# Last slices of the output chunk tile by tile, seam gate slices on VectorE, and an opening in one-slice stages

## The chip, the cores and the metric

The kernel runs on one core of a Trainium2 chip. TensorE multiplies, VectorE and ScalarE work on elements, GpSimd and SyncE issue DMAs. The metric is the device time of one execution in microseconds; lower is better. The order of work on each engine is fixed in the program; engines wait for each other at semaphores.

## The reference

One denoising step of a two-layer backbone on 384 tokens: 128 context tokens and 256 latent tokens, model width 2048, all in float32. Both kinds of token share the weights, and differ in the conditioning vector:

```
mod = SiLU(cond) @ w_ada[l] + b_ada[l] -> shift, scale, gate
h   = RMSNorm_pre(x) * (1 + scale) + shift
p   = h @ w_in[l]                       (5120 columns)
l=0: windowed attention with sink, and a 2-D DFT mixing
l=1: multi-scale pooling, and chunked spatial gating
every branch * SiLU(its gate path), concatenated: o (2048 wide)
x   = x + gate * RMSNorm_post(o @ w_out[l])
```

The outputs are the new x of both kinds of token, and the keys and values of the context tokens in layer 0.

## The kernel before, in words

**Tiles and chunks.** The tokens are three tiles of 128 (t = 0 to 2). The product is worked off in 28 chunks of 512 output columns (`CHUNKS`): per layer ten of w_in and four of w_out ("out" chunks; those are chunks 10 to 13 and 24 to 27). Layer 1 begins at chunk L1 = 14. A chunk takes 16 k-steps, one for each slice of 128 rows (`KT`). A weight is split in a high and a low half of its bits: ScalarE rounds (`round_half`, L938, writes `w_hi`), VectorE subtracts (`split_half`, L1147, writes `w_lo`), for two slices at a time, called a half. A k-step is nine products, three for each tile (L732 to L734), into the accumulator bank of that tile; `mm_done` counts halves. `w_hi` and `w_lo` are rings of three halves. The loop of the k-step takes all three tiles within a step, so the three tiles of a chunk are complete together.

**The timetable.** `timetable()` writes down by hand at which place (chunk, step) every other piece of work stands, and each engine goes through the same list of places. At a place TensorE does the k-step and then the entries; ScalarE and VectorE do the entries and then the round or the split of the half that lies two ahead (from chunk 3 on; in the opening the round and split stand first). `pre` entries stand ahead of a chunk. Side products (transposes of h, the gate rows, and so on) take turns in two spare banks. SyncE loads the weights in the order of `loads`, through a ring `raw` of four slots of 1 MB; a load waits until the one four before it has been used, and everything behind waits too.

**The opening.** Chunks 0 to 2 (v, k, q) run interleaved, as h comes slice by slice. h needs the scale and shift columns of its slice, which come from a product of `w_ada` with the condition: eight stages (`STAGES`) of two slices, each of four entries `first_ada` (L754, one load of 1 MB in runs of 256 columns for scale and for shift, ring of three slots), transposed by `first_cols` (L761), and then `h`: transposes on TensorE (L800), scale and shift on ScalarE (L1006), its high half (L1010), its low half on VectorE (L1358). Chunks 1 and 2 share a bank set, so their sums are spilled to SBUF at each change (`spill`, 24 times).

**Wide sums.** The gate of layer 0 and the shift of layer 1 are not multiplied on TensorE. VectorE sums them (`wide_sum`, L1313): GpSimd loads half rows of w_ada into two buffers `wide_raw` (L627), each used by two sums; the next load into a buffer waits for both. 64 sums a block, one in 1.3 steps for the gate (from chunk 3 step 10) and one a step for the shift (from chunk 9 step 3). `wide_fold` adds the partitions up at the end.

**The seam.** Between the last out chunk of layer 0 (13) and chunk 14: the shift's transposes `cols` (L791), then for all three tiles the square of the sums (`square_y`, L977), the product with the gate (`evac`, L1443), the mean and root, the `residual` (L1194, twelve pieces of 512 columns), the squares of the new x (L951), the pre-norm (L1177), and h. The gate of layer 1 starts here: slices 0 to 5 (`SEAM_ADA`) are products on TensorE (L693), the other ten are ten loads into `raw` summed on VectorE in two halves (`lane_sum`, L1345, 40 sums, one in 2.5 steps from chunk 15). x is loaded again (`reload`) at step 6 of chunk 13. The end of chunk 27 has the same chain, and then the stores.

Of the kernel before, what the change touches and what calls it, by code (L numbers as in the profile page):

```python
# [29 lines left out]
P = 128  # L30
D = 2048
# [31 lines left out]
L1 = PER_LAYER  # L63

# [6 lines left out]
SEAM_ADA = 6  # L71
# [9 lines left out]
STAGES = 8  # L81

WIDE = [(GATE_BLOCK[0], FIRST, 10, 13, 10), (SHIFT_BLOCK, FIRST + 6, 3, 1, 1)]
# [3 lines left out]
HALVES = [half for q in range(4) for half in (  # L87
    [(1, 0), (0, 0), (1, 1), (0, 1), (2, 0), (2, 1)] if q == 0 else
    [(0, 2 * q), (1, 2 * q), (1, 2 * q + 1), (0, 2 * q + 1), (2, 2 * q), (2, 2 * q + 1)])]
HALVES += [(c, h) for c in range(FIRST, len(CHUNKS)) for h in range(KT // 2)]  # L90
NTH_HALF = {ch: n for n, ch in enumerate(HALVES)}
QUARTERS = []
for c_, h_ in HALVES:
    if (c_, h_ // 2) not in QUARTERS:
        QUARTERS.append((c_, h_ // 2))
NTH_QUARTER = {cq: n for n, cq in enumerate(QUARTERS)}
# [12 lines left out]
def timetable():  # L109
# [12 lines left out]
    steps = [(c, 2 * h + i) for c, h in HALVES[:FIRST * KT // 2] for i in range(2)]  # L122

    def first(n, *entry):
        put(*steps[n], *entry)

    pre(0, "square")
    for i in range(4):
        pre(0, "first_ada", 0, i)
        if i == 1:  # L130
            pre(0, "norm")
    pre(0, "first_weights")
    pre(0, "first_cols", 0)
    for k in range(2):
        pre(0, "h", 0, k)
    for i, n in enumerate((0, 1, 2, 2)):
        first(n, "first_ada", 1, i)
    first(3, "first_cols", 1)
    for k in range(2, 4):
        first(3, "h", 0, k)  # L140
    for b in range(2, STAGES):
        at_ = 12 * (b // 2 - 1) + 4
        ada, cols, h = ((0, 1, 2, 4), 5, 6) if b % 2 == 0 else ((5, 6, 7, 8), 9, 10)
        for i in range(4):
            first(at_ + ada[i], "first_ada", b, i)
        first(at_ + cols, "first_cols", b)
        for k in range(2 * b, 2 * b + 2):
            first(at_ + h, "h", 0, k)
    for c in SPILLED:
        for q in range(4):  # L150
            for t in range(TOKS):
                put(c, 4 * q + 3, "spill", c, q, t)

    pre(L1, "cols", SHIFT_BLOCK)
    for t in range(TOKS):
# [11 lines left out]
    for c, (layer, kind, _) in enumerate(CHUNKS):  # L167
        nxt = c + 1
        if kind == "out":

            for n in range(2):
                put(c, 10 + 2 * n, "gate_y", c, n)
            if c not in (L1 - 1, 2 * L1 - 1):
                for t in range(TOKS):
                    put(nxt, t, "evac", c, t)
            continue
        step = {"k": 3, "q": 3, "vd": 2}.get(kind, 1)
        if c == KEPT:

            for t in range(TOKS):  # L180
                put(FIRST - 1, 12 + t, "evac", c, t)
            continue
        if c == SPILLED[0]:

            for n, t in ((-2, 1), (0, 2)):
                first(len(steps) - 4 + n, "evac", c, t)
            for n, t in ((-1, 0), (0, 1), (2, 2)):
                first(len(steps) - 4 + n, "turn", c, t)
            continue
# [40 lines left out]
    for half in range(2):  # L230
        for i in range(SUM_LOADS):
            for j in range(4):
                n = 4 * (SUM_LOADS * half + i) + j
                put(L1 + 1, 5 * n // 2, "lane_sum", half, i, j // 2, j % 2)
        put(L1 + 1, 10 * SUM_LOADS * (half + 1) + 2, "fold", half)
    put(10, 5, "cols", SCALE_BLOCK)
    end = len(CHUNKS)
    for t in range(TOKS):
        pre(end, "evac", end - 1, t)
    pre(end, "residual", 1)  # L240
# [8 lines left out]
def places():  # L249
    yield ("pre", 0)  # L250
    for c, h in HALVES:
        if h == 0 and c >= FIRST:
            yield ("pre", c)
        for s in range(2 * h, 2 * h + 2):
# [4 lines left out]
def hybrid_step(nc, x_prompt, x_sample, cond_cols, w_ada, first_cols, ada_rows, norm_rows, w_in, w_out, cache_kt,  # L259
# [10 lines left out]
    loads, fetched = [], 2  # L270
    for p in places():
        if p[0] == "at" and p[2] % 2 == 0:
            n = NTH_HALF[p[1], p[2] // 2] + (3 if p[1] < FIRST else 2)
            if n < len(HALVES):
                c, h = HALVES[n]
# [1350 lines left out]
```

## Time and profile before

| | |
|---|---|
| median of 3 runs | 1205.12 us (1203.51 to 1207.18) |
| the profiled execution | 1205.11 us |
| its span, first to last instruction | 1203.3 us |
| TensorE busy | 1136.3 us, 94% |
| VectorE busy | 694.0 us, 58% |
| ScalarE busy | 421.5 us, 35% |
| mean granted TensorE clock | 0.987 of full speed |
| DMA | 235.97 MB, mean 196 GB/s |

The time of an execution is the span and about 1.8 us around it. An engine that is busy is not an engine at its peak: a product counts as busy while it waits in TensorE's pipeline. "Idle before" in a row, in square brackets, is the time that the engine stood still ahead of that instruction, and what released it. Times in a timeline are counted from the start of the span.

### The profile page before, as it was taken

The page shows a single profiled execution, that of the slowest core. Times are in us where ns is not written, and L with a number is a line of the kernel's source. Part 1 is how long each engine was busy: PE and PEld are TensorE (multiplying, and loading weights), DVE is VectorE, ACT ScalarE, POOL GpSimd, SP SyncE. Part 2 cuts the span into 40 slices and gives each one's busy share as a digit, 9 for nine tenths or more (in the row PEclk, how much of TensorE's full clock was granted, in tenths as well). Part 3 has the DMA queues.
Part 4 walks back from the last instruction along what each step waited for, and adds up shares of the span by engine and source line. Part 5 has one row for each costly group of instructions (what it writes and reads, how often), then busy time and mean ns, then how long its engine had stood idle before and what let it go on. Part 6 is the DMA issues. An engine that isn't in the chain of part 4 may idle for free.

```text
span 1203.3 us, 13779 instructions
## 1 busy us (share of the span) xinstructions
PE 1136.3 (94%) x5404; PEld 876.3 (73%) x5404; DVE 694.0 (58%) x949; ACT 421.5 (35%) x653; POOL 50.9 (4%) x98
## 2 busy tenths in 40 slices
PE   3799999999999999999999699999999999999994
PEld 0456677877787877777777388888788878878883
DVE  3354555678788784688873553466665643243333
ACT  3323234333455342233332673223233323242331
POOL 1000010000000001011111000000000000000000
PEclk9999999999999999999999799999999999999998
DMA  9998974655565576666678534444344633433413
GB/s 329 328 315 295 301 253 151 227 202 196 180 245 210 183 263 245 210 215 222 221 241 310 226 106 146 150 158 161 125 173 171 209 114 131 140 105 107 138 35 105
DMA packets 113056, 235.97 MB, mean 196 GB/s; under 512 B 5280, under 2 KB 38080, under 8 KB 109408
## 3 DMA queue, kind: packets, MB, share of 16 engines
q1 hardware_dynamic: 100976, 190.86, 46.1%
q0 software_dynamic: 11440, 41.08, 10.3%
q10 hardware_dynamic: 576, 3.16, 0.7%
q8 instruction: 43, 0.70, 0.2%
q14 instruction: 21, 0.17, 0.0%
HBM read 231.40 MB, written 3.67 MB: 195 GB/s over the span
## 4 chain that ended last, share of the span: by engine, by line
PE 82%; DMA 7%; DVE 6%; issue 2%; ACT 2%; SPq 0%; DVEq 0%; ACTq 0%
PE bank L732 23%; PE bank L734 22%; PE bank L733 22%; DMA wide_raw<-in_w_ada 5%; PE bank L754 3%; DVE wide L1313 2%; DVE w_lo L1147 2%; PE bank L856 1%; DVE x L1194 1%; PE bank L693 1%; DMA raw_first<-in_w_ada 1%; PE bank L839 1%; DMA raw<-in_w_in 1%; PE bank L901 1%; PE bank L800 1%
## 5 line engine op out<-in xcount | busy, mean ns | idle before, releaser
L732 PE MATMUL bank<-w_hi,h_op 128*128 128x512 f32 x1152 | 474.7, 412 | 7.2 <-DVE h_op L1358 4.2
L734 PE MATMUL bank<-w_hi,h_op 128*128 128x512 f32 x1152 | 452.9, 393 | 0.0
L733 PE MATMUL bank<-w_lo,h_op 128*128 128x512 f32 x1152 | 451.6, 392 | 0.0
L1147 DVE TENSOR_TENSOR w_lo<-raw,w_hi 128x1024 fp32r<-128x1024 f32 x224 | 272.9, 1221 | 196.6 <-ACT w_hi L938 196.3
L938 ACT ACTIVATE w_hi<-raw 128x1024 fp32r<-128x1024 f32 x224 | 234.7, 1054 | 244.5 <-PE bank L734 233.0
L732 PEld LDWEIGHTS bank<-w_hi,h_op 128*128 128x128 f32 x1152 | 217.8, 189 | 87.3 <-issue 40.5
L734 PEld LDWEIGHTS bank<-w_hi,h_op 128*128 128x128 f32 x1152 | 217.5, 189 | 48.6
L733 PEld LDWEIGHTS bank<-w_lo,h_op 128*128 128x128 f32 x1152 | 218.2, 189 | 40.5 <-issue 0.7
L1313 DVE SCALAR_TENSOR_TENSOR wide<-wide_raw,cond,wide 128x1024 f32<-128x1024 f32 x120 | 152.3, 1276 | 20.0 <-DMA wide_raw<-in_w_ada 19.8
L732 PE MATMUL bank<-w_hi,o_low 128*128 128x512 f32 x192 | 76.9, 400 | 3.1 <-DVE w_lo L1147 3.0
L734 PE MATMUL bank<-w_hi,o_low 128*128 128x512 f32 x192 | 74.9, 390 | 0.0
L733 PE MATMUL bank<-w_lo,o_low 128*128 128x512 f32 x192 | 74.9, 390 | 0.0
L754 PE MATMUL bank<-raw_first,cond 128*32 128x512 f32 x256 | 38.0, 672 | 22.0 <-DMA raw_first<-in_w_ada 19.8
L1006 ACT ACTIVATE silu<-bank,shift_t,scale_t 128x128 f32<-128x128 f32 x64 | 29.1, 505 | 67.6 <-PE bank L800 58.3
L627 POOL DMA_DIRECT2D wide_raw<-in_w_ada x64 | 33.9, 530 | 363.0 <-DVE wide L1313 330.4
L732 PEld LDWEIGHTS bank<-w_hi,o_low 128*128 128x128 f32 x192 | 36.0, 188 | 14.2 <-DVE w_lo L1147 6.5
L1345 DVE SCALAR_TENSOR_TENSOR lanes<-raw,cond,lanes 128x1024 f32<-128x1024 f32 x36 | 46.0, 1278 | 0.0
L1358 DVE TENSOR_TENSOR h_op<-silu,h_op 128x384 fp32r<-128x384 f32 x32 | 17.9, 558 | 47.8 <-ACT h_op L1010 47.8
L734 PEld LDWEIGHTS bank<-w_hi,o_low 128*128 128x128 f32 x192 | 36.0, 188 | 7.7
L733 PEld LDWEIGHTS bank<-w_lo,o_low 128*128 128x128 f32 x192 | 36.1, 188 | 6.9
L1025 ACT ACTIVATE probs_t<-bank 128x384 f32<-128x384 f32 (+1 forms) x36 | 15.1, 419 | 64.8 <-PE bank L846 64.6
L1032 ACT ACTIVATE probs<-bank,neg_max 128x384 f32<-128x384 f32 (+1 forms) x36 | 18.4, 511 | 50.9 <-DVE neg_max L1381 50.9
(181 smaller groups left out, 755.6 us busy)
## 6 DMA issues: line engine op xcount, KB each, us to landing
raw<-in_w_in SPq DMA_DIRECT2D x80, 1024.0 KB, 6.7
raw_first<-in_w_ada SPq DMA_DIRECT2D x64, 512.0 KB, 6.2
raw<-in_w_ada SPq DMA_DIRECT2D x32, 1024.0 KB, 5.7
wide_raw<-in_w_ada POOLq DMA_DIRECT2D x64, 512.0 KB, 4.3
raw<-in_w_out SPq DMA_DIRECT2D x32, 1024.0 KB, 5.1
x<-in_x_sample SPq DMA_DIRECT2D x2, 1024.0 KB, 9.7
x<-in_x_sample ACTq DMA_DIRECT2D x2, 1024.0 KB, 11.4
out_y_sample<-x SPq DMA_DIRECT2D x8, 256.0 KB, 3.1
```

The lines of the kernel that those rows point to most:

```text
L627: pool.dma_start(wide_raw[:, i % 2, :], w_ada[layer, k * P:(k + 1) * P, col:col + LANES])\
L732: pe.matmul(out, operand(layer, kind, 0, k, t), hi, start=k % group == 0, stop=False)
L733: pe.matmul(out, operand(layer, kind, 0, k, t), lo, start=False, stop=False)
L734: last = pe.matmul(out, operand(layer, kind, 1, k, t), hi, start=False, stop=k % group == group - 1)
L754: last = pe.matmul(out[32 * j:32 * j + 32, :], cond[:, 4 * i + j, :], raw_first[:, slot, CW * j:CW * (j + 1)], start=True, stop=True)
L938: act.activation(w_hi[:, half % WRING, :, :].rearrange("p k n -> p (k n)"), src, ACT.Copy)\
L1006: last = act.activation(full[:, lo_:hi_], side_bank(e)[:, lo_:hi_], ACT.Identity, bias=shift_t[:, k, c_:c_ + 1], scale=scale_t[:, k, c_:c_ ...
L1032: freed(act.activation(probs[:, 0:n], side_bank(e)[:, 0:n], ACT.Exp, bias=neg_max[:, u:u + 1], scale=SCALE, accum_out=row_sum[:, u:u + 1]), e)
L1147: dve.tensor_tensor(w_lo[:, half % WRING, :, :].rearrange("p k n -> p (k n)"), src, hi, ALU.subtract)\
L1313: dve.scalar_tensor_tensor(out=wide[:, c_, cols], in0=src, scalar=cond[:, k, c_:c_ + 1], in1=wide[:, c_, cols], op0=ALU.mult, op1=ALU.add)\
L1345: dve.scalar_tensor_tensor(out=lanes[:, c_, :], in0=src, scalar=factor, in1=lanes[:, c_, :], op0=ALU.mult, op1=ALU.add).then_inc(lane_summ ...
L1358: dve.tensor_tensor(h_op[:, 1, k, :], h_full[k % 2], h_op[:, 0, k, :].bitcast(F32), ALU.subtract)\
```

## The change

Four things are changed.

1. *Opening.* The first two slices have a stage each, so there are nine stages: `[0], [1], [2, 3], ...`. A stage of one slice has two entries, each of eight slices of w_ada and 128 columns for scale and shift; they multiply 256 columns instead of 512. Weights of chunks 0 to 2 are loaded by halves (`UNITS`, 512 KB, one slot of `raw` each). The order within a round of two slices is chunk 2, 0, 1 and 1, 0, 2 in turn; the first round goes slice by slice. There are 27 spills (`STAYS`). The order of the first loads is written out. The norm stands before the first entry, and a Sqrt on ScalarE between the squares of x loads its table early.
2. *Wide sums.* The gate block takes one sum in 1.2 steps; the shift block begins at chunk 8 step 13 and takes one in 1.1 steps.
3. *Last slices.* In chunks 13 and 27 the last four slices are multiplied tile by tile: `tile_steps` does 12 products of tile 0 at step 12, of tile 1 at 13, of tile 2 at 14. It counts `y_done`. Squares, gate product, root and residual are entries for each tile, and in chunk 13 so are the squares of x. The gate rows come at steps 7 and 9 instead of 10 and 12, the Sqrt table at step 10, the shift's `cols` at step 8 of chunk 13. The rounds and splits of the first two halves of chunk 14 are entries of their own.
4. *Seam gate.* `SEAM_ADA` is 2: two slices on TensorE, and 14 in 14 loads and 56 lane sums, one in 2.25 steps.

```diff
-SEAM_ADA = 6
+SEAM_ADA = 2
-WIDE = [(GATE_BLOCK[0], FIRST, 10, 13, 10), (SHIFT_BLOCK, FIRST + 6, 3, 1, 1)]
+WIDE = [(GATE_BLOCK[0], FIRST, 10, 12, 10), (SHIFT_BLOCK, FIRST + 5, 13, 11, 10)]
+STAGES = [[0], [1]] + [[2 * r, 2 * r + 1] for r in range(1, ROUNDS)]
+OPENING = [(2, 0), (0, 0), (2, 1), (0, 1), (1, 0), (1, 1)]
+OPENING += [(c, 2 * r + i) for r in range(1, ROUNDS) for c in round_order(r) for i in range(2)]
...
     pre(0, "square")
+    pre(0, "norm")
+    pre(0, "first_ada", 0, 0)
+    pre(0, "norm_rest")
+    pre(0, "first_ada", 0, 1)
     pre(0, "first_cols", 0)
+    pre(0, "first_weights", 0)
+    pre(0, "h", 0, 0)
+    pre(0, "first_weights", 1)
+    pre(0, "first_ada", 1, 0)
+    first(0, "first_ada", 1, 1)
+    first(1, "first_cols", 1)
+    first(1, "h", 0, 1)
+    for n, i in ((1, 0), (1, 1), (3, 2), (4, 3)):
+        first(n, "first_ada", 2, i)
+    first(4, "first_cols", 2)
...
+    for b in range(3, len(STAGES)):
+        at_ = 6 * (b - 2)
         for i in range(4):
+            first(at_ - 1 + i, "first_ada", b, i)
+        first(at_ + 3, "first_cols", b)
+        for k in STAGES[b]:
+            first(at_ + 4, "h", 0, k)
...
-    pre(L1, "cols", SHIFT_BLOCK)
-    for t in range(TOKS):
-        pre(L1, "evac", L1 - 1, t)
-    pre(L1, "residual", 0)
+    put(L1 - 1, 8, "cols", SHIFT_BLOCK)
+    after = [NTH_HALF[L1, h] for h in range(2)]
+    for layer, c in enumerate(LAST):
+        put(c, 10, "table", c)
+        put(c, 12, "y_square", c, 0)
+        put(c, 12, "y_mix", c, 0)
+        put(c, 12, "y_root", layer, 0)
+        put(c, 12, "residual", layer, 0)
+        put(c, 13, "y_square", c, 1)
+        if layer == 0:
+            put(c, 13, "round", after[0])
+        put(c, 13, "y_mix", c, 1)
+        put(c, 14, "y_root", layer, 1)
+        put(c, 14, "residual", layer, 1)
+        put(c, 14, "y_square", c, 2)
+        put(c, 14, "y_mix", c, 2)
+        if layer == 0:
+            pre(c + 1, "x_square", 0)
+        pre(c + 1, "y_root", layer, 2)
+        pre(c + 1, "residual", layer, 2)
+    pre(L1, "x_square", 1)
+    pre(L1, "round", after[1])
+    pre(L1, "x_square", 2)
+    pre(L1, "x_norm")
+    pre(L1, "xn", 1, 0)
     pre(L1, "ada", GATE_BLOCK[1], 0, SEAM_ADA)
-    pre(L1, "xn", 1, 0)
-    for k in range(3):
+    pre(L1, "split", after[0])
+    pre(L1, "h", 1, 0)
+    pre(L1, "split", after[1])
+    for k in range(1, 3):
         pre(L1, "h", 1, k)
...
-                put(c, 10 + 2 * n, "gate_y", c, n)
+                put(c, (7 if c in LAST else 10) + 2 * n, "gate_y", c, n)
...
+            def tile_steps(c, t):
+                layer, kind, _ = CHUNKS[c]
+                out = acc(c, t)[:, :]
+                for k in range(KT - 4, KT):
+                    half = NTH_HALF[c, k // 2]
+                    hi = w_hi[:, half % WRING, k % 2, :]
+                    lo = w_lo[:, half % WRING, k % 2, :]
+                    pe.matmul(out, operand(layer, kind, 0, k, t), hi, start=False, stop=False)
+                    pe.matmul(out, operand(layer, kind, 0, k, t), lo, start=False, stop=False)
+                    last = pe.matmul(out, operand(layer, kind, 1, k, t), hi, start=False, stop=k == KT - 1)
+                    if t == TOKS - 1 and k % 2:
+                        last.then_inc(mm_done, 1)
+                if t < TOKS - 1:
+                    last.then_inc(y_done, 1)
...
+                if c in LAST and k >= KT - 4:
+                    if k == KT - 4:
+                        pe.wait_ge(lo_ready, half + 2)
+                    if k < KT - 1:
+                        tile_steps(c, k - (KT - 4))
+                    return
```

## Rows read from the trace of the kernel before

**Rows 1.** The page: the span, and its busy time by engine.
```profile
span 1203.3 us, 13779 instructions
...
PE 1136.3 (94%) x5404; PEld 876.3 (73%) x5404; DVE 694.0 (58%) x949; ACT 421.5 (35%) x653; POOL 50.9 (4%) x98
```

**Rows 2.** Waits of TensorE, whole span: total us, times, longest us.
```profile
PE bank L732 <- DVE w_lo L1147: 5.9, 9, 2.0
```

**Rows 3.** Timeline, TensorE (start, us, instruction): gate product, chunks 10, 13, 24, 27.
```profile
536.21 0.49 PE L814 MATMUL bank<-gate_parts,row_sel_r 32*128 32x512 f32 x1
...
648.92 0.49 PE L814 MATMUL bank<-gate_parts,row_sel_r 32*128 32x512 f32 x1
...
1074.21 0.49 PE L814 MATMUL bank<-gate_parts,row_sel_r 32*128 32x512 f32 x1
...
1176.12 0.49 PE L814 MATMUL bank<-gate_parts,row_sel_r 32*128 32x512 f32 x1
```

**Rows 4.** Chain of waits, 500 to 660 us: start us, us, what.
```profile
514.37 6.37 DMA wide_raw<-in_w_ada
...
597.39 1.22 DVE w_lo L1147
598.61 1.21 DVE wide L1313
600.10 6.70 DMA wide_raw<-in_w_ada
...
619.86 5.21 DMA wide_raw<-in_w_ada
```

**Rows 5.** Timelines of TensorE and ScalarE at the seam.
```profile
660.36 0.60 PE L791 MATMUL bank<-ident,rows 128*128 128x128 f32 x4
...
661.22 1.28 ACT L975 ACT_TABLE_LOAD   x1
662.51 0.20 ACT L975 ACTIVATE junk<-stat 128x3 f32<-128x3 f32 x1
...
676.25 0.19 ACT L951 ACTIVATION_READ_ACCUMULATOR mixed<-x 128x1 f32 x1
...
681.90 0.77 PE L732 MATMUL bank<-w_hi,h_op 128*128 128x512 f32 x1 [0.34 <-DVE h_op L1358]
```

**Rows 6.** Timeline of the end of the last chunk and the tail.
```profile
1178.28 1.23 DVE L1147 TENSOR_TENSOR w_lo<-raw,w_hi 128x1024 fp32r<-128x1024 f32 x1 [5.80 <-ACT w_hi L938]
...
1187.33 0.39 PE L734 MATMUL bank<-w_hi,h_op 128*128 128x512 f32 x1
...
1188.83 2.13 DVE L1443 TENSOR_TENSOR mixed<-bank,silu 128x512 f32<-128x512 f32 x3 [9.32 <-ACT junk L977]
...
1191.72 8.04 DVE L1194 SCALAR_TENSOR_TENSOR x<-mixed,stat,x 128x512 f32<-128x512 f32 x12
```

**Rows 7.** Timeline of the opening.
```profile
16.58 1.94 PE L754 MATMUL bank<-raw_first,cond 128*32 128x512 f32 x8 [16.58 <-DMA raw_first<-in_w_ada]
...
25.59 1.94 PE L754 MATMUL bank<-raw_first,cond 128*32 128x512 f32 x8 [1.06 <-DMA raw_first<-in_w_ada]
...
28.20 1.06 ACT L938 ACTIVATE w_hi<-raw 128x1024 fp32r<-128x1024 f32 x1 [2.56 <-DMA raw<-in_w_in]
...
30.92 1.06 ACT L938 ACTIVATE w_hi<-raw 128x1024 fp32r<-128x1024 f32 x1 [1.66 <-DMA raw<-in_w_in]
...
36.04 0.76 PE L732 MATMUL bank<-w_hi,h_op 128*128 128x512 f32 x1 [1.75 <-DVE h_op L1358]
```

**Rows 8.** Timeline of TensorE, later in the opening: entry products.
```profile
79.03 1.06 PE L754 MATMUL bank<-raw_first,cond 128*32 128x512 f32 x8 [0.72 <-ACT silu L1006]
...
82.29 1.07 PE L754 MATMUL bank<-raw_first,cond 128*32 128x512 f32 x8
...
154.11 1.07 PE L754 MATMUL bank<-raw_first,cond 128*32 128x512 f32 x8 [0.72 <-ACT silu L1006]
```

**Rows 9.** Waits of TensorE from 700 to 1190 us.
```profile
PE bank L732 <- DVE w_lo L1147: 0.5, 1, 0.5
```

More of the change, by code:

```diff
@@ L118, in pre @@
         at.setdefault(("pre", c), []).append(entry)
-    steps = [(c, 2 * h + i) for c, h in HALVES[:FIRST * KT // 2] for i in range(2)]
     def first(n, *entry):
-        put(*steps[n], *entry)
+        put(*OPENING[n], *entry)
     pre(0, "square")
[L128 to L132, printed above, removed]
-    pre(0, "first_cols", 0)
[L134 to L137, printed above, removed]
@@ L180, in timetable @@
             for t in range(TOKS):
-                put(FIRST - 1, 12 + t, "evac", c, t)
+                put(FIRST - 1, 14 + t // 2, "evac", c, t)
             continue
         if c == SPILLED[0]:
[L185 to L188, printed above, removed]
+            first(-4, "evac", c, 1)
+            first(-3, "turn", c, 0)
+            first(-2, "evac", c, 2)
+            first(-2, "turn", c, 1)
+            put(FIRST, 0, "turn", c, 2)
             continue
@@ L233, in timetable @@
                 n = 4 * (SUM_LOADS * half + i) + j
-                put(L1 + 1, 5 * n // 2, "lane_sum", half, i, j // 2, j % 2)
-        put(L1 + 1, 10 * SUM_LOADS * (half + 1) + 2, "fold", half)
+                put(L1 + 1, 9 * n // 4, "lane_sum", half, i, j // 2, j % 2)
+        put(L1 + 1, 9 * SUM_LOADS * (half + 1) + 2, "fold", half)
     put(10, 5, "cols", SCALE_BLOCK)
[L237 to L240, printed above, removed]
     return at
@@ L250, in places @@
     yield ("pre", 0)
[L251 to L254, printed above, removed]
+    for c, s in OPENING:
+        yield ("at", c, s)
+    for c in range(FIRST, len(CHUNKS)):
+        yield ("pre", c)
+        for s in range(KT):
             yield ("at", c, s)
@@ L266, in hybrid_step, with opening_loads @@
     assert len(nth_side) == len(side)
-    loads, fetched = [], 2
+    def opening_loads():
+        yield from (("first_ada", 0, 0), ("first_ada", 0, 1), ("mm", 0), ("mm", 1))
+        yield from (("first_ada", 1, 0), ("first_ada", 1, 1), ("mm", 2))
+        yield from (("first_ada", 2, 0), ("first_ada", 2, 1), ("mm", 3), ("first_ada", 2, 2), ("first_ada", 2, 3))
+        yield from (("mm", 4), ("mm", 5), ("first_ada", 3, 0))
+        for b in range(3, len(STAGES)):
+            for i in range(1, 4):
+                yield ("mm", 3 * (b - 1) + i - 1)
+                yield ("first_ada", b, i)
+            if b + 1 < len(STAGES):
+                yield ("first_ada", b + 1, 0)
+    loads = list(opening_loads())
+    fetched = 3 * ROUNDS
     for p in places():
@@ L287, in hybrid_step @@
                 loads.append(("sum", e[1], e[2]))
-    assert [x[1] for x in loads if x[0] == "mm"] == list(range(len(QUARTERS)))
+    assert [x[1] for x in loads if x[0] == "mm"] == list(range(len(UNITS)))
+    assert [x for x in loads if x[0] == "first_ada"] == [e for e in side if e[0] == "first_ada"]
     nth_first = {x: n for n, x in enumerate(x for x in loads if x[0] == "first_ada")}
@@ L498, in half_ahead @@
         def half_ahead(p):
-            if p[0] == "at" and p[2] % 2:
+            if p[0] == "at" and p[2] % 2 and p[1:] not in ((L1 - 1, KT - 3), (L1 - 1, KT - 1)):
                 half = NTH_HALF[p[1], p[2] // 2] + 2
@@ L1510, in part @@
                     norm_x(0)
-                    for j in range(PIECES):
+                    norm_piece(0)
+                elif what == "norm_rest":
+                    for j in range(1, PIECES):
                         norm_piece(j)
```

278 lines of the change are left out of this document (156 added, 122 removed).

## The prediction

> **What bounds the kernel now.** I read the page first: the span is 1203.3 us [rows 1], and the profiled execution's own time is 1205.11 us, so 1.8 us lie outside the span; the median of the three runs is 1205.12, the same. I add everything against 1205.1. TensorE holds 94% of the span [rows 1], so only stretches in which it stands still or is pushed apart can pay. The list of what TensorE waits for [rows 2] names one inside the steady run: `w_lo`, the low half of a weight split, late from VectorE, 5.9 us in nine waits. The list shows no more of it, because products that run one by one behind late weight loads count as busy; the rate shows the whole.
>
> The steady rate comes from TensorE's timeline [rows 3]. The gate product after step 10 of an output chunk recurs in layer 1 from 1074.21 to 1176.12 over three chunks: 33.97 us a chunk. Two gate products cost about 0.5 each, so a k-step is 2.06 us, and a third of four steps (one tile's share) 2.75. In layer 0 the same three intervals take 648.92 - 536.21 = 112.71 us: 10.8 more. The fold of the shift block (about 2.1) is work; 8.7 is loss, and some 0.9 is lost just before 536. So **9.6 us** go at the wide sums of the shift block. Why: the chain of waits [rows 4] runs there 12 times, from 514.37 to 619.86, through the same ring: load, sum, split, sum, next load. 11 turns take 105.5 us, 9.6 each; less two sums (1.28 each), a split (1.22) and about 0.5 of latencies, 5.3 us are left for a load; a turn holds four sums, placed one a step, for which TensorE would want only 4 x 2.12 = 8.5.
>
> The two other losses are read from the timelines: the seam, from the last product of layer 0 (660.36) to the first of layer 1 (681.90), 21.5 us [rows 5], and the tail, from 1187.56 (1187.33 plus one spacing of 0.23) to the end of the span, 15.7 us [rows 6]. In both, ScalarE and VectorE do a serial chain after all three tiles are complete. The opening takes 36.04 us to the first main product [rows 7].
>
> **Opening.** Four entries of one megabyte, then two of w_in, land before the first product. Entries with 1 KB runs land 9.01/3 = 3.00 us apart (16.58 to 25.59), w_in with 2 KB runs 2.72 apart [rows 7]. The new first stage needs two entries and two half-megabyte loads. Its entries have 512-byte runs, which no row shows. A price per byte plus one per packet through the two rows gives 0.28 us for 512 packets more, and for 1024 more 0.6: 3.6 us an entry. Lower bound 3.0 (runs cost nothing), upper bound 6.0 (all cost is per packet). I take 3.6, as going from 2 KB to 1 KB shows so little. The Trainium skill's "DMA: Bandwidth & Descriptors", under Specifications, gives 512 B as the smallest transfer at line rate; by it the entries cost 3.0 and the opening gains up to 2.6 us more. No run shown here decides it.
>
> x is in at 16.6 - 3.0 = 13.6. Entries at 17.2 and 20.8, two weight halves (1.36 each) 23.5, third entry 27.1. The third entry's product stands in TensorE's order ahead of the first k-step and takes 2.0 us, so the first step begins at 29.1; the h chain is done by 27. That is 7 us earlier. Then the loads set the pace: fourth entry 30.7, a weight half 32.1, stage 2's entries at 35.1, 38.1, 42.5, 45.5, two halves 48.2, and stage 3's at 51.2, 55.6, 60.0 and 64.3. TensorE waits about 1 us at each of the last three. Its product ends at 65.4; three steps with their column and h transposes and one more entry product (3 x 2.06, 1.1, 1.0 and 0.2 behind each fp32 group) put the thirteenth step at about 74. Before, it follows the product at 82.29, at 83.4 [rows 8]. But 13 entries are done by then instead of 15: two more at 1.2 us each remain. The waits of 0.72 us for ScalarE, one at each odd stage [rows 8], lie at an h transpose with no step behind it; the new order puts a step there, and the two that fall after step 12 go. 9.4 - 2.4 + 1.4 = 8.4; with small slips for three more spills I take **8.0** (2 to 11). A round needs 16.1 us of loads and had 75.08/4 = 18.8 us of TensorE, so after stage 3 the loads fall behind no more. Half-size weight loads leave four halves in the ring, over 16 us of work, so the ring costs nothing.
>
> **Shift block.** It starts at chunk 8 step 13 instead of chunk 9 step 3, one sum in 1.1 steps, and ends at the same place. Four sums then have 4.4 x 2.12 = 9.3 us. The turn of 9.6 comprises two sums, one split between them and the load. The new places alternate in blocks of ten sums: even sums on odd steps, where the split falls between, and on even ones, where it follows and the turn is 1.2 shorter, 8.4. The mean, 9.0, fits; the odd blocks overrun by 0.3 a turn, which the two halves of lead absorb. So the stall goes but for 0.6: **9.0** (4 to 9.6). The gate block of layer 0 goes from 1.3 to 1.2 steps a sum; that costs some VectorE room in the attention stage and perhaps 0.3.
>
> **Last four slices by tile.** TensorE's work is the same, in other order. Count from its end, T. Tile 0 is complete at T - 5.5, tile 1 at T - 2.75. Before, VectorE's product follows T by 1.27 us [rows 6]: square and its latency. A tile on VectorE now costs reduce and scale 0.36, product 0.71, reciprocal 0.2, residual 8.04/3 = 2.68: 3.95. Tile 0 runs from -4.2 to -0.25; tiles 1 and 2 queue behind it to 3.7 and 7.7. Before, the residual ended at 1199.76, T + 12.2: 4.5 us gained. What follows (the last 256 KB out, 3.5 us) stays.
>
> A price comes with it. TensorE now wants both halves 6 and 7 split before step 12, at T - 8.24. The gate products move to steps 7 and 9. After the second (0.4 before step 10, T - 12.8) ScalarE has to empty it, round half 6, load the Sqrt table and use it (661.22 to 662.71, 1.5 [rows 5]), and only then round half 7. Round 7 waits behind these on ScalarE, VectorE's split behind round 7, TensorE behind the split. Before, the split of half 7 ended 3.39 us after the gate product (1176.12 to 1179.51 [rows 3, 6]); with one round more (1.06 [rows 7]) and the table it ends 5.95 after, at T - 6.85. TensorE stands for 1.4 us, in both last chunks (bounds 0, if ScalarE gets ahead, and 3). ScalarE's next instruction starts 0.01 us behind a table load here [rows 5]. The Trainium skill's "ScalarE: Activation LUTs", under What ACT_TABLE_LOAD costs, adds a drain of 1380 ns to the load of 1283; by it the stall would be 2.8 us, and the whole sum 2.8 us worse. The trace has the load at 1.28 and no room for the drain, and I go by the trace.
>
> Tail: 4.5 - 1.4 = 3.1, taken as **3.0** (1 to 5).
>
> Seam: the residual is done at 7.7; ScalarE squares tile 1 from 4.3 to 6.4, rounds a half to 7.5, squares tile 2 in two halves to 9.9. From the end of the last square to the first product took 681.90 - 676.44 = 5.46 [rows 5]; one small add more (0.2), and the 0.6 evacuation of the gate block now comes after the norm pieces. First product at T + 15.0 instead of 21.5: 6.5. Off go 1.4 of stall and 0.6 for the shift's transposes [rows 5], which lay in the gap and now lie among the steps. **4.5** (1 to 6). The gate block's products at the seam fall from six slices to two. They ran inside the gap, hidden behind the residual; in the shorter gap six would have ended at about 12 and been next in line, so that move earns nothing alone, but protects the 4.5. x's reload, issued at the same step 6, has to have landed by T - 2.8.
>
> **Sixteen more lane sums** (1.28 each, 20.5 us) go to VectorE in chunks 15 to 22, one per 2.25 steps. VectorE is 58% busy over the span [rows 1] and TensorE waited 0.5 us for splits in all after 700 [rows 9], so they cost perhaps 0.5.
>
> Sum: 8.0 + 9.0 + 3.0 + 4.5 - 0.8 = 23.7; 1205.1 - 23.7 = 1181.4.
>
> **Rivals.**
> *The runs of 512 bytes are dear.* At 6.0 an entry the first four cost 9.6 more: 1191. For it: the opening is paced by loads. Against: 1 KB costs only a tenth more than 2 KB. 0.12.
> *The shift block still starves.* If the load, not the placing, sets the turn (9.6 against 9.3 of cover, loads up to 6.7 [rows 4]), half or all of the 9 stays: 1186 to 1190. 0.16.
> *The tiles gain nothing.* The late half 7, or x late, eats the seam and tail: 1186 to 1189. 0.08.
> *Everything fits better:* entries at 3.0, ScalarE ahead: 1176. 0.09.
> *Slower.* The ring of `raw`: a sum load holds one of four slots for 6.75 steps until its fourth sum, and SyncE's queue waits behind it. There are 14 instead of 10. If each kept the weights back for 2 us, 28 us would go in chunks 15 to 22, and 1209 would result; from that price on it decides. Against: the load behind it is wanted some 5 steps, 10 us, later, and with ten such loads TensorE waited 0.5 us in all [rows 9]. 0.04. No change that can be told, because several of these meet: 0.04.
> The forecast itself: 0.47.
>
> 0.3% is 3.6 us, about what this kernel's measurement tells from no change. Faster 0.91, same 0.04, slower 0.05 (the ring and an unseen thing). Range: the likeliest alone is 1177 to 1186; with the dear runs, the starving block and the better case, 1173 to 1192.
>
> **What would show it.** First main product near 29 us instead of 36; thirteenth step near 74. Three gate intervals in layer 0 of about 104 us instead of 112.7, and the wide loads gone from the chain. A gap of about 15 us at the seam, a tail of about 11.2 after the last product, and a pause of 1 to 2 us before step 12 of both last chunks, waiting for `w_lo`. The forecast is wrong if entries of the first stages land over 4.5 us apart, if the chain still runs through `wide_raw`, or if the last residual begins later than T + 6.

## The result and the profile after

The changed kernel takes 1184.87 us (median of 4 runs, 1183.69 to 1185.8), the kernel before 1204.32 beside it (4 runs, 1200.76 to 1207.18). The ratio is 0.9839 [0.9811, 0.9868]: 19.5 us, 1.6% less. The profiled executions, by which everything below goes, have spans of 1203.3 and 1181.6 us, 21.7 apart.

The page after, span and busy time by engine (before: [rows 1]):

```profile
span 1181.6 us, 13864 instructions
...
PE 1126.5 (95%) x5404; PEld 876.4 (74%) x5404; DVE 715.6 (61%) x985; ACT 421.4 (36%) x660; POOL 50.9 (4%) x98
```

TensorE is busy 9.8 us less. Of this 5.4 lie in the gap at the seam, where four slices of the gate fewer are multiplied, 3.4 in the opening and 2.5 between the gate product of chunk 10 and the end of chunk 13; elsewhere it is busy 1.4 more. The other 12 us are idle time that went.

What TensorE waits for, whole span (total us, times, longest us); before the only row of the steady run was [rows 2]:

```profile
PE bank L838 <- DMA raw_first<-in_w_ada: 24.8, 10, 16.9
PE bank L884 <- DVE mixed L1276: 8.6, 1, 8.6
PE bank L814 <- DVE w_lo L1243: 2.6, 3, 2.0
PE bank L769 <- DVE w_lo L1243: 2.6, 2, 1.3
```

Row 1 is the opening, row 2 the seam. In row 3, L814 is a k-step's product, and one wait of 2.0 us in chunk 18 is most of it; in row 4, L769 is the first product of `tile_steps`, and each of its two waits is one of 1.3 us.

TensorE's timeline at the landmarks (start, us, instruction, idle before and its releaser): the opening, the gate product of chunks 10, 11, 12 and 13, the last chunk of layer 0, the seam, one wait in chunk 18, and the last chunk.

```profile
16.94 1.94 PE L838 MATMUL bank<-raw_first,cond 128*32 128x256 f32 x16 [16.94 <-DMA raw_first<-in_w_ada]
20.44 1.94 PE L838 MATMUL bank<-raw_first,cond 128*32 128x256 f32 x16 [1.57 <-DMA raw_first<-in_w_ada]
...
28.75 0.80 PE L814 MATMUL bank<-w_hi,h_op 128*128 128x512 f32 x1
...
72.38 1.07 PE L838 MATMUL bank<-raw_first,cond 128*32 128x512 f32 x8
...
139.18 1.06 PE L838 MATMUL bank<-raw_first,cond 128*32 128x512 f32 x8 [0.65 <-DMA raw_first<-in_w_ada]
...
530.99 0.49 PE L898 MATMUL bank<-gate_parts,row_sel_r 32*128 32x512 f32 x1
...
564.95 0.49 PE L898 MATMUL bank<-gate_parts,row_sel_r 32*128 32x512 f32 x1
...
598.92 0.49 PE L898 MATMUL bank<-gate_parts,row_sel_r 32*128 32x512 f32 x1
...
640.22 0.47 PE L769 MATMUL bank<-w_hi,h_op 128*128 128x512 f32 x1 [1.30 <-DVE w_lo L1243]
...
648.56 1.92 PE L752 MATMUL bank<-raw,cond 128*32 128x512 f32 x16
...
662.29 0.77 PE L814 MATMUL bank<-w_hi,h_op 128*128 128x512 f32 x1 [0.34 <-DVE h_op L1469]
...
864.78 0.50 PE L814 MATMUL bank<-w_hi,h_op 128*128 128x512 f32 x1 [2.05 <-DVE w_lo L1243]
...
1162.84 0.47 PE L769 MATMUL bank<-w_hi,h_op 128*128 128x512 f32 x1 [1.27 <-DVE w_lo L1243]
```

The first product stands at 28.75 instead of 36.04 [rows 7]. The gate products of the shift block are 33.96 and 33.97 us apart, the rate of layer 1 before. Layer 0 ends at T = 648.47 (last tile product and one spacing) instead of 660.36 [rows 5], and the first product of layer 1 follows 13.8 us later instead of 21.5. The last product ends at 1171.13, 10.5 us before the end of the span; before, 15.7 [rows 6]. The waits in square brackets at 640.22, 864.78 and 1162.84 are time that the changed kernel lost anew.

Put end to end, the 21.7 us of span are (T is the end of the last product of layer 0):

| stretch | before | after | gain |
|---|---|---|---|
| to the start of the last spill, taken as the end of the opening | 187.81 | 181.15 | 6.7 |
| to the gate product of chunk 10 | 348.40 | 349.84 | -1.4 |
| to the end T of chunk 13 | 124.15 | 117.48 | 6.7 |
| T to first product of layer 1 | 21.54 | 13.82 | 7.7 |
| layer 1 to its last product | 505.66 | 508.84 | -3.2 |
| tail | 15.74 | 10.47 | 5.3 |

The tiles at the seam, VectorE's timeline of chunk 13's end:

```profile
638.85 1.23 DVE L1243 TENSOR_TENSOR w_lo<-raw,w_hi 128x1024 fp32r<-128x1024 f32 x1 [1.39 <-ACT w_hi L1022]
...
645.26 2.74 DVE L1300 SCALAR_TENSOR_TENSOR x<-mixed,stat,x 128x512 f32<-128x512 f32 x4
...
649.08 2.74 DVE L1300 SCALAR_TENSOR_TENSOR x<-mixed,stat,x 128x512 f32<-128x512 f32 x4
...
652.91 2.74 DVE L1300 SCALAR_TENSOR_TENSOR x<-mixed,stat,x 128x512 f32<-128x512 f32 x4
```

The residuals of the three tiles stand 3.8 us apart, tile 0's before T, the last one done at 655.65, T + 7.2. At the end of the last chunk it is the same, and there the one residual of 8.04 us ended at T + 12.2 before [rows 6].

### The profile page after: what moved, and what is told of

Same layout as the page of the kernel before. It is cut to its first block, busy times and chain, and to the rows that moved or that the text cites. A ratio compares the mean times of both kernels' runs of the same rounds, so it can differ in the third digit from the quotient of the medians.

```text
span 1181.6 us, 13864 instructions
## 1 busy us (share of the span) xinstructions
PE 1126.5 (95%) x5404; PEld 876.4 (74%) x5404; DVE 715.6 (61%) x985; ACT 421.4 (36%) x660; POOL 50.9 (4%) x98
## 4 chain that ended last, share of the span: by engine, by line
PE 81%; DVE 5%; DMA 5%; ACT 4%; issue 3%; SPq 2%; DVEq 0%; ACTq 0%
PE bank L814 23%; PE bank L816 23%; PE bank L815 23%; DMA raw_first<-in_w_ada 4%; DVE w_lo L1243 2%; PE bank L940 1%; SPq L615 1%; PE bank L752 1%; ACT w_hi L1022 1%; ACT silu L1087 1%; DVE x L1300 1%; PE bank L838 1%; PE bank L923 1%; PE bank L985 1%; PE bank L890 1%
## 5 line engine op out<-in xcount | busy, mean ns | idle before, releaser
L814 PE MATMUL bank<-w_hi,h_op 128*128 128x512 f32 x1128 | 464.7, 412 | 3.1 <-DVE w_lo L1243 2.6
L816 PE MATMUL bank<-w_hi,h_op 128*128 128x512 f32 x1128 | 443.8, 393 | 0.0
L815 PE MATMUL bank<-w_lo,h_op 128*128 128x512 f32 x1128 | 442.3, 392 | 0.0
L814 PEld LDWEIGHTS bank<-w_hi,h_op 128*128 128x128 f32 x1128 | 213.2, 189 | 79.9 <-issue 35.3
L816 PEld LDWEIGHTS bank<-w_hi,h_op 128*128 128x128 f32 x1128 | 212.7, 189 | 46.9
L815 PEld LDWEIGHTS bank<-w_lo,h_op 128*128 128x128 f32 x1128 | 213.6, 189 | 39.8 <-issue 0.7
L814 PE MATMUL bank<-w_hi,o_low 128*128 128x512 f32 x192 | 75.9, 396 | 0.0
L1456 DVE SCALAR_TENSOR_TENSOR lanes<-raw,cond,lanes 128x1024 f32<-128x1024 f32 x52 | 66.4, 1277 | 0.0
L838 PE MATMUL bank<-raw_first,cond 128*32 128x512 f32 (+1 forms) x288 | 36.8, 598 | 25.1 <-DMA raw_first<-in_w_ada 24.8
L1087 ACT ACTIVATE silu<-bank,shift_t,scale_t 128x128 f32<-128x128 f32 x64 | 29.1, 505 | 80.3 <-PE bank L884 60.9
L1469 DVE TENSOR_TENSOR h_op<-silu,h_op 128x384 fp32r<-128x384 f32 x32 | 17.9, 558 | 43.2 <-ACT h_op L1091 43.2
L814 PEld LDWEIGHTS bank<-w_hi,o_low 128*128 128x128 f32 x192 | 36.1, 188 | 8.0 <-issue 0.8
```

What stands on the lines that cost most here:

```text
L814: pe.matmul(out, operand(layer, kind, 0, k, t), hi, start=k == begin, stop=False)
L815: pe.matmul(out, operand(layer, kind, 0, k, t), lo, start=False, stop=False)
L816: last = pe.matmul(out, operand(layer, kind, 1, k, t), hi, start=False, stop=k == end)
L838: last = pe.matmul(out[32 * j:32 * j + 32, 0:n_], cond[:, ks * i + s, :], raw_first[:, slot, n_ * s:n_ * (s + 1)], start=s < 4, stop=s >= ...
L1087: last = act.activation(full[:, lo_:hi_], side_bank(e)[:, lo_:hi_], ACT.Identity, bias=shift_t[:, k, c_:c_ + 1], scale=scale_t[:, k, c_:c_ ...
L1456: dve.scalar_tensor_tensor(out=lanes[:, c_, :], in0=src, scalar=factor, in1=lanes[:, c_, :], op0=ALU.mult, op1=ALU.add).then_inc(lane_summ ...
```

## The experiments

Ten runs. The change's own time was taken a second time among them, as a base for small differences. Where one is compared with the changed kernel, it is with 1184.87 for the first four runs (experiments 1 to 3) and with the second time, 1184.64, for those after it. The kernel before took 1206.52 us beside the first four, 1202.84 beside the next ones and 1203.54 beside the last two, against 1204.32 beside the changed kernel; so a difference of 2 to 3 us between times that were not taken side by side isn't told by them alone, and the profiles are asked where it lies.

**1. The wide sums alone, and all but them.** The kernel before with the new places, and the changed kernel with the old ones:

```diff
-WIDE = [(GATE_BLOCK[0], FIRST, 10, 13, 10), (SHIFT_BLOCK, FIRST + 6, 3, 1, 1)]
+WIDE = [(GATE_BLOCK[0], FIRST, 10, 12, 10), (SHIFT_BLOCK, FIRST + 5, 13, 11, 10)]
```

> The kernel before with the two lines of wide sums of the change alone (gate block one sum in 1.2 steps, shift block from chunk 8 step 13 at one in 1.1). Theory (the turn of load, two sums and a split was longer than four steps, and its slack was the whole loss): the three gate intervals in layer 0 fall from 112.7 to about 104.0 us, the attention stage loses about 1 to 1.5 us, and the time falls by 7 to 8 us. Rival (the load time sets the turn whatever the places): the intervals stay above 110 and the time falls by under 3 us.

> The changed kernel with the wide sums as before (1.3 steps, then from chunk 9 step 3 one a step). Theory: the gate intervals of layer 0 are about 110 to 113 us again, the time from the end of the opening to the first gate product of chunk 10 is 1 to 1.5 us shorter than in the changed kernel, and the time is 6 to 8 us above it. Rival (the lead of the new opening has its own part in the cure): the intervals stay near 104 and the time within 2 us.

Measured: alone 1194.51 us, ratio 0.9905 [0.9884, 0.9927], 12.0 less than the kernel before beside it, where 7 to 8 were expected; undone 1193.01, ratio 0.9896 [0.9869, 0.9923], 8.1 above the changed kernel. Alone, the timeline of TensorE shows the gate products of chunks 10 and 13 at the same step as before:

```profile
534.06 0.49 PE L814 MATMUL bank<-gate_parts,row_sel_r 32*128 32x512 f32 x1
...
638.09 0.49 PE L814 MATMUL bank<-gate_parts,row_sel_r 32*128 32x512 f32 x1
```

104.03 us against 112.71 [rows 3]: 8.7 gained there. Some 2.5 more by the end of the opening is the same opening at 185.36 instead of 187.81, which is scatter. Undone, the changed kernel needs 129.0 us from the gate product of chunk 10 to T instead of 117.5, and gets 1.3 back ahead of that product and 1.0 in layer 1. Of these 11.5 us some 3 are the clock's: behind a wait of 2.53 us it was granted at half speed for about 7 us. So the places themselves are worth 8 to 9 us both ways. TensorE's waits (whole span) have the row back:

```profile
PE bank L814 <- DVE w_lo L1243: 7.5, 6, 2.5
```

So with the same loads the places of the sums decide whether TensorE stalls, and the rival of a block that starves anyway falls from both sides.

**2. Tiles in the step again.** The changed kernel with the entries of each tile, but its products in the old order, so that all tiles are complete together:

```diff
-                if c in LAST and k >= KT - 4:
-                    if k == KT - 4:
-                        pe.wait_ge(lo_ready, half + 2)
-                    if k < KT - 1:
-                        tile_steps(c, k - (KT - 4))
-                    return
...
+                    if c in LAST and k == KT - 1 and t < TOKS - 1:
+                        last.then_inc(y_done, 1)
```

> The changed kernel with the last four slices of chunks 13 and 27 multiplied step by step as before, so that all three tiles are complete in the last step; the entries for each tile stay. Theory (the order of the products is what gains, as VectorE's chain of 3.8 us a tile starts 5.5 us earlier): the tail is 5 us longer than 10.5, the gap at the seam 5 us longer than 13.8, the pauses of 1.3 us before step 12 go, and the time is 7 to 8 us above the changed kernel. Rival (the finer entries gain by themselves, squares of x beside the residual above all): the seam loses less than 3 us and the time less than 4 us.

Measured: 1189.93 us, ratio 0.987 [0.9847, 0.9893], 5.1 slower than the changed kernel, less than the 7 to 8 expected and more than the rival's 4. TensorE's timeline at the seam:

```profile
649.67 0.39 PE L809 MATMUL bank<-w_hi,h_op 128*128 128x512 f32 x1
649.99 1.92 PE L752 MATMUL bank<-raw,cond 128*32 128x512 f32 x16
...
667.80 0.77 PE L807 MATMUL bank<-w_hi,h_op 128*128 128x512 f32 x1 [0.34 <-DVE h_op L1464]
```

The seam gap is 667.80 - 649.90 = 17.9 us (13.8 + 4.1), the tail 14.5 (10.5 + 4.1), and neither `w_lo` pause is there. So of the 7.7 us gained at the seam 4.1 come from the order of the products, and 3.6 from the rest of the change there; at the tail it is 4.1 and 1.2. The 3.6 aren't all the cut in entries: before, the first square of the sums stood behind the shift's transposes and the table load,

```profile
662.75 0.60 ACT L977 ACTIVATE junk<-bank 128x512 f32<-128x512 f32 x1
```

at T + 2.4, while at the tail, where the table was in already, it stood at T + 0.55. In this run it stands at 648.80, T - 1.1, as it waits for its own tile alone. That the transposes and the table left the gap is thus worth up to 1.8 of the 3.6; the two were not tried apart. The order, with the table at step 10, costs two pauses and gives 8.2.

**3. The Sqrt table later.** The changed kernel, the table behind the last round:

```diff
-        put(c, 10, "table", c)
+        put(c, 12, "table", c)
```

> The changed kernel with the Sqrt table loaded at step 12 of chunks 13 and 27, behind the round of half 7, instead of at step 10. Theory (the load of 1.3 us and the small Sqrt stand ahead of that round and make TensorE wait 1.3 us before step 12): both pauses go, seam gap and tail stay as they are, as the table is in before tile 0 is complete; 2.0 to 2.6 us gained. Rival (the gate product at step 9 alone makes the round late): pauses of over 0.8 us stay. Second rival (the load is then in the way of tile 0's square): the tail grows by what the pause gives.

Measured: 1181.44 us, ratio 0.9798 [0.9777, 0.9819], 3.4 faster than the changed kernel, where 2.0 to 2.6 were expected. ScalarE's timeline, of the changed kernel and then of this one:

```profile
634.66 0.60 ACT L1175 ACTIVATE silu<-bank 128x512 f32<-128x512 f32 x1 [2.30 <-PE bank L898]
635.15 1.05 ACT L1022 ACTIVATE w_hi<-raw 128x1024 fp32r<-128x1024 f32 x1
636.22 1.28 ACT L1189 ACT_TABLE_LOAD   x1
637.52 0.20 ACT L1189 ACTIVATE junk<-stat 128x3 f32<-128x3 f32 x1
637.75 1.06 ACT L1022 ACTIVATE w_hi<-raw 128x1024 fp32r<-128x1024 f32 x1
```

```profile
635.27 2.00 ACT L1022 ACTIVATE w_hi<-raw 128x1024 fp32r<-128x1024 f32 x2
637.29 1.28 ACT L1189 ACT_TABLE_LOAD   x1
638.59 0.20 ACT L1189 ACTIVATE junk<-stat 128x3 f32<-128x3 f32 x1
641.99 0.60 ACT L1058 ACTIVATE junk<-bank 128x512 f32<-128x512 f32 x1 [3.20 <-PE bank L771]
```

The two rounds stand together, both pauses are gone, and the table is in 3.2 us before the first square wants it. The seam (13.84) and the tail (10.41) stay as they are. The pauses are 2.6 of the 3.4. Most of the rest is not the table's: layer 1 is 2.3 us shorter, 1.3 of it the pause, and about 0.8 because TensorE's clock didn't fall behind the wait in chunk 18, as it did in both profiles of the changed kernel (see the last section).

**4. The fold before its successors.** The first seven of 14 lane loads are folded by a product on TensorE at place 65 of chunks 15 on; the first sum of the second half stands at place 63:

```diff
-        put(L1 + 1, 9 * SUM_LOADS * (half + 1) + 2, "fold", half)
+        put(L1 + 1, 9 * SUM_LOADS * (half + 1) - 1, "fold", half)
```

> The changed kernel with the fold of each half of the lane sums three steps earlier (at 62 and 125 steps after the start instead of 65 and 128). Theory (the first lane sum of the second half, at step 63, waits for the fold on TensorE at step 65, and the split of that step lies behind it on VectorE, so that TensorE waits 2.05 us at 864.8): that wait goes and the time falls by 2 us. Rival (sixteen more lane sums crowd VectorE): a wait for a late low half of 1 us or more stays in chunks 15 to 23.

> The changed kernel itself, for its time on the same chip as the next three: a ratio of 0.981 to 0.987 to the kernel before, a span near 1182 us.

Measured: 1181.98 us, ratio 0.9825 [0.981, 0.984], against 1184.64, ratio 0.985 [0.9834, 0.9866], for the changed kernel again: 2.7 less. VectorE's timeline of the changed kernel at the wait:

```profile
862.83 0.75 DVE L1454 TENSOR_SCALAR lanes<-raw,cond 128x1024 f32<-128x1024 f32 x1 [10.56 <-issue]
863.50 1.22 DVE L1243 TENSOR_TENSOR w_lo<-raw,w_hi 128x1024 fp32r<-128x1024 f32 x1
```

VectorE stands 10.6 us before the first sum of the second half. The profile names no releaser; by the program it is the fold, as `lanes` may not be written anew before TensorE has read it. The split of the next weights is queued behind the sum, and TensorE, which finishes the wait only by getting to place 65, then lacks that split for 2.05 us. With the fold three steps earlier TensorE's waits from 700 to 1180 us are down to the pause before step 12 of chunk 27:

```profile
PE bank L769 <- DVE w_lo L1243: 1.3, 1, 1.3
```

The crowding by sixteen more sums, the rival, had no part in it, nor had the ring of `raw`: all 14 loads are there still, and the wait is gone. Every time of this run lies below every time of the changed kernel beside it (1180.57 to 1182.71 against 1183.45 to 1186.7). Of the 2.7 us 2.05 are the wait. Some 0.8 are TensorE's clock, which was granted at half speed (1.2 GHz) for 3 us behind that wait in both profiles of the changed kernel. In experiment 5 the wait is there and the clock stays at full speed. Three us of each, 1.2 us behind the restart (us; PE, PEld, VectorE, ScalarE, GpSimd busy; clock, DMA share, GB/s):

```profile
866.00:869.00 3.00, 3.00 (x8) 2.31 (x8) 3.00 (x5) 0.96 (x2) 0.00 (x0) 0.51 0.93 316
```

```profile
863.36:866.36 3.00, 3.00 (x14) 2.46 (x14) 3.00 (x5) 0.97 (x2) 0.00 (x0) 1.00 0.90 315
```

It is 8 products against 14 in the same time.

**5. Entries ahead of the weights.** In the opening SyncE issues three entries of a stage each behind a weight half. Turned round:

```diff
-                yield ("mm", 3 * (b - 1) + i - 1)
                 yield ("first_ada", b, i)
+                yield ("mm", 3 * (b - 1) + i - 1)
```

> The changed kernel with entries 1 to 3 of stages 3 to 8 each loaded ahead of the weight half with which they are paired, instead of behind it. Theory (SyncE's queue stands at the weight half, which waits for a slot of the ring of four half-filled slots, and the entries behind it start late): the waits of TensorE for an entry in stages 4 to 8 (0.2 to 0.65 us each, 2.1 in all) go, and the time falls by about 2 us. Rival (the DMA engines are full, and any order gives the same): the waits stay at 2 us in sum or move to the weights.

Measured: 1180.25 us, ratio 0.9812 [0.9798, 0.9826], 4.4 less than the changed kernel, where about 2 were expected. SyncE's timeline, of the changed kernel and of this one (L648 a weight half, L615 an entry, in two DMAs):

```profile
66.83 0.37 SPq L648 DMA_DIRECT2D raw<-in_w_in  x1
67.24 1.02 SPq L615 DMA_DIRECT2D raw_first<-in_w_ada  x2
75.19 0.37 SPq L648 DMA_DIRECT2D raw<-in_w_in  x1
```

```profile
66.53 1.42 SPq L648 DMA_DIRECT2D raw<-in_w_in  x1
72.39 0.92 SPq L615 DMA_DIRECT2D raw_first<-in_w_ada  x2
74.08 0.37 SPq L648 DMA_DIRECT2D raw<-in_w_in  x1
```

The changed kernel's queue issues nothing from 68.3 to 75.2: it stands at a weight half whose slot is still in use, with entries behind it for which there would be room. TensorE's waits from 50 to 165 us, of the changed kernel and of this one:

```profile
PE bank L838 <- DMA raw_first<-in_w_ada: 3.7, 7, 1.0
```

```profile
PE bank L838 <- DMA raw_first<-in_w_ada: 1.0, 1, 1.0
```

The opening ends at 177.58, against 181.15 and 182.28 in the two profiles of the changed kernel, and none of the eight profiles with this opening and the old order of loads ends it before 180.70. The waits that went are 2.7 us of this; where the rest lies was not broken down. Had the DMA engines been short of time, the turn would have moved the waits to the weights; it removed them. The stretch from 65 to 80 us says the same, of the changed kernel and of this one (columns as above):

```profile
65.00:80.00 15.00, 15.00 (x80) 9.60 (x80) 7.15 (x12) 5.56 (x9) 0.00 (x0) 1.00 0.92 294
```

```profile
65.00:80.00 15.00, 15.00 (x80) 9.67 (x79) 7.12 (x13) 5.71 (x9) 0.00 (x0) 1.00 1.07 355
```

The engines moved 294 GB/s while the queue stood, and 355 when it did not.

**6. Six slices of the gate at the seam.** The last part of the change undone. With six slices the splits of chunk 14's first halves stand ahead of the product, since the fourth load of w_ada needs a slot that they free:

```diff
-SEAM_ADA = 2
+SEAM_ADA = 6
...
     pre(L1, "x_square", 2)
+    pre(L1, "split", after[0])
+    pre(L1, "split", after[1])
...
-    pre(L1, "split", after[0])
     pre(L1, "h", 1, 0)
-    pre(L1, "split", after[1])
```

> The changed kernel with six gate slices on TensorE at the seam and ten on VectorE, as before; the splits of the first two halves of chunk 14 stand ahead of the norm, since loads 4 to 6 need the slot of those weights. Theory (the loads of the last three can only start when those splits are done, some 8 us after the last product of chunk 13, and take 2.7 us each): the gap at the seam grows from 13.8 to 22 to 26 us and the time by 8 to 12 us. Rival (the six products stay hidden behind the residual as in the kernel before): the gap stays within 2 us of 13.8, and the move of the slices is worth nothing.

Measured: 1192.86 us, ratio 0.9919 [0.9903, 0.9935], 8.2 more than the changed kernel. TensorE's timeline at the seam:

```profile
649.28 2.78 PE L752 MATMUL bank<-raw,cond 128*32 128x512 f32 x24
663.60 1.93 PE L752 MATMUL bank<-raw,cond 128*32 128x512 f32 x8 [11.54 <-DMA raw<-in_w_ada]
...
672.41 0.47 PE L814 MATMUL bank<-w_hi,h_op 128*128 128x512 f32 x1 [0.69 <-DVE h_op L1469]
```

The gap is 23.2 us, longer than before the change. Three slices run at once; the fourth has no slot until a split of chunk 14's weights, which now waits for the residuals of three tiles (the splits end at 658.63). Its load then lands at 663.60 and the last one at 668.55, long after the norm. Of the 9.4 us by which the gap grew layer 1 gives 1.1 back.

**7. The opening alone.** The kernel before with the new stages, order, half-size loads, 27 spills and early norm, and nothing else.

> The kernel before with the opening of the change alone (stages, order, spills, loads, early norm). Theory (the opening starts 7.2 us earlier and loses some of it again to entries held up behind weight halves): the first product near 28.8 us, the last spill at 181 to 184 us, seam 21.5, tail 15.7, gate intervals near 112.7, and the time 4 to 6 us below the kernel before (ratio 0.995 to 0.997). Rival (the earlier start goes through whole): 7 us or more. Second rival (the lead is eaten in the shift block, where the wide loads set the pace): the last spill is 5 us earlier, and the time falls by less than 2 us.

Measured: 1200.19 us (12 runs), ratio 0.9975 [0.9959, 0.999]: 3 us, less than the 4 to 6 expected. Its opening ends at 182.25, as in the changed kernel (181.15 and 182.28). The old shift block takes some of that back, as the second rival has it, though not so much: the chain of waits from 440 to 660 us runs through the wide loads still, and one of them takes longer than any of [rows 4]:

```profile
557.89 6.83 DMA wide_raw<-in_w_ada
...
606.28 6.20 DMA wide_raw<-in_w_ada
```

From the gate product of chunk 10 to T this kernel takes 126.0 us, 1.8 more than the kernel before.

**8. The three mends together** (3, 4 and 5 in one kernel):

> The changed kernel with the three mends together: the Sqrt table at step 12, the fold of the lane sums three steps earlier, entries ahead of the weight halves. They lie in different stages, so they should add: 2.8 us of pauses, 2.0 of the fold's wait and 4.4 of the opening, some 9 us in all: a ratio of 0.975 to 0.979 to the kernel before, a span near 1173 us. Rival (the loads that come earlier in the opening or the changed places move waits elsewhere): less than 7 us below the changed kernel.

Measured: 1175.63 us (6 runs, 1174.12 to 1176.75), ratio 0.9767 [0.9742, 0.9791]: 9.0 us faster than the changed kernel, and 28 faster than before. Seam (13.84) and tail (10.41) are unchanged, TensorE waits for `w_lo` 0.8 us in the whole span. Singly the mends gave 3.4, 2.7 and 4.4, together 10.5; the 0.8 of the clock stands in both of the first two. Layer 1 takes 504.26 us here, against 508.84 in the changed kernel and 505.66 before.

## Why the prediction was right, and where it was off

Forecast 1181.4 us (1173 to 1192), measured 1184.87: inside the range, and inside the narrower 1177 to 1186, 3.5 us above. The mechanisms were the ones named; the opening, the stretch behind it, the seam, the tail and layer 1 were of another size. That the sum is so near is in part luck: the seam and the tail gave 2.3 us more than their terms, and the others 4.1 less.

**Opening: 8.0 predicted, 6.7 measured, 5.5 in the second profile.** Even this is uncertain by its base: the old opening ends at 187.81 and 185.36 in two profiles, the new one between 180.70 and 183.49 in eight, 4.6 apart on the mean. Its start went by the working: entries 3.50 us apart (16.94 to 20.44; 3.6 taken), first product 28.75 (29.1), the entry product ahead of the thirteenth step at 72.38 and the step at 73.4 (74). What failed is "after stage 3 the loads fall behind no more" with "Half-size weight loads leave four halves in the ring, over 16 us of work, so the ring costs nothing". Four half loads in the ring of `raw` do cover TensorE, but that ring makes the queue wait, and what is behind it in SyncE's order are the entries, with their own ring free. The sum compared bytes and did not go through the queue in order. TensorE's waits for entries after 66 us (2.1 us in five) show it, and the turned order gives 4.4 us: with it the opening ends 10.2 us before the old one's 187.81. The rival of dear 512-byte runs fell with the 3.50.

**Shift block: 9.0 predicted; 8.7 measured alone.** Undoing it costs 11.5 in the block, of which the clock is some 3, and 8.1 in all. Right in place and size: 33.96 us a chunk, three intervals in 104.03 (104 predicted), no wide load in the chain. The rival of a block that still starves is refuted.

**To the gate product of chunk 10: 1.4 lost,** where about nothing was forecast (9.0 for the block less the 8.7 of the intervals, and 0.3 off for the gate block's sums). With the new opening and the old places this stretch is 0.2 to 0.3 longer than before (348.57 with the places undone, 348.69 with the opening alone), with the new places and the old opening 0.3 (348.70), and with both 1.2 to 2.1 in eight profiles (349.60 to 350.48). Why the two together cost more than each wasn't tried and stays open.

**Seam: 4.5 predicted net.** The gap was to be 15.0 and is 13.8, so 7.7 less than before. Nearly all of the 1.2 lies ahead of the last square: the third tile's residual is done at T + 7.2 (7.7), as a tile takes VectorE 3.83 us and not 3.95, and the last square ends at 657.23, T + 8.8 (9.9). From there to the first product it took 5.1, as worked out. The pause of 1.4 was there with 1.30. Net it is 5.8.

**The move of the gate slices** was costed at nothing alone, as "six would have ended at about 12 and been next in line". That it protects the gap is right; but what is next in line is not TensorE's time but a slot of `raw`, and six slices in the new seam cost 8.2 us.

**Tail: 3.0 predicted net (4.5 - 1.4);** measured 5.3 and a pause of 1.27: 4.0. The last residual ends at 1178.30, T + 7.2 (7.7), and from there to the end of the span it takes 3.3 (3.5).

**The pauses before step 12,** 1 to 2 us, waiting for `w_lo` in both last chunks: 1.30 and 1.27, and by the mechanism named, the table between two rounds on ScalarE. Here the Trainium skill's "ScalarE: Activation LUTs", under What ACT_TABLE_LOAD costs, was set against the trace; by its drain they would, as an estimate, have been 2.8. The trace decided: the Activate stands 0.02 us behind the end of the load (637.52), the load 0.02 us behind the round, and the pauses are 1.3.

**Layer 1: not in the sum but for 0.5.** It became 3.2 us longer: 1.27 the pause, 2.05 the wait in chunk 18 and some 0.8 the clock behind it, less about 1 us that the rest of the layer became shorter. The sentence that failed is the one on sixteen more lane sums: they were priced as busy time of an engine at 58%, "so they cost perhaps 0.5". Busy time was no matter; one sum stood two steps ahead of the product that frees its buffer. The old wait of 0.5 [rows 9] was the same thing, small: VectorE stood 6.58 us before the sum at 854.39, released by the fold, and TensorE waited at 857.97.

Added up by terms: opening 1.3 less, the stretch to chunk 10 1.4 less, layer 1 1.4 less (1.9 lost without the pause, 0.5 forecast), against 1.3 more at the seam and 1.0 at the tail. That is 1.8 of the 2.0 us by which the spans fall short of the 23.7 (21.7). The other 1.5 of the 3.5 is in how the profiled executions stand to the medians: 1205.12 less 1184.87 is 20.2.

## What to carry to other kernels

A load queue that issues in order is to be simulated entry by entry, with all rings it serves: the ring that is full stops the loads of the ring that is empty, and to count bytes against time does not show it. When work is moved to an engine with room, look for what each moved piece waits for and what is queued behind it, not for its busy share. And when a chain after the last product is cut by tiles, the order of the products pays by itself (4.1 us at this seam and at the tail), and so does what is taken out of the gap and waits for one tile alone (3.6 and 1.2 us). The last preparations of the weights have to stand ahead of everything that the tiles want; here that was two pauses of 1.3 us.

## What the runs showed of the hardware

Loads of one megabyte in 512-byte runs land 3.50 us apart (3.40 to 3.50 in ten profiles), against 3.00 in 1 KB and 2.72 in 2 KB runs [rows 7]: cheap, but not free. The Trainium skill's "DMA: Bandwidth & Descriptors", under Specifications, puts line rate at 512 bytes and above; the runs here show it 14% below the 1 KB rate.

The opening, with the loads that it hangs on, ends at different times in executions of the same code (180.70 to 183.49 in eight profiles; with the old code 187.81 and 185.36), so up to 2.8 us of an opening can't be told by one profile.

TensorE's clock is granted at one of two levels here, full (2.4 GHz) or half (1.2 GHz). At the seam TensorE stands 8.6 us; the clock is at half speed when it begins layer 1 and full 2.4 us later, where it took 4.8 us before the change. A single wait in a stretch that is otherwise busy can do it too. Twelve waits of 1.8 to 2.53 us for `w_lo` stand in the profiles, and the clock fell behind four of them: for some 3 us behind the wait of 2.05 us in both profiles of the changed kernel and of 2.14 us in experiment 6, and for 7 us behind 2.53 us with the places undone. Behind the other eight (1.8 to 2.05 us) it stayed full, four of them the same wait for the fold in chunk 18, and it did so behind the pauses of 1.3 us. What decides stays open. The fall in chunk 18 costs some 0.8 us: to the gate product of chunk 24 layer 1 takes 393.93 us in both profiles of the changed kernel and 392.82 to 393.13 in the four without.
